# Last mask ahead of the w_down issues, a transposing DMA at positions 6 to 14

## What is computed

```python
def rmsnorm(x, g):
    y = x32 * lax.rsqrt(jnp.mean(x32 * x32, axis=-1, keepdims=True) + EPS) * g
...
def block(x, ...):
    u, q, k, v, o, ig, lf = mixer_inputs(x, norm1, w_in, b_gate)   # rmsnorm(x, norm1) @ w_in
    pool_out = pool_mix(u_ext, pos, w_pool, pool_scale)            # windows 2, 4, 8, 16
    h, mstate = run_mlstm(q, k, v, ig, lf)                         # chunked matrix memory, 4 heads of 128
    x = x + mixer_output(pool_out, h, o, head_gain, w_out, x.dtype)
    x = x + channel_mixer(x, norm2, w_up, w_down)                  # relu(rmsnorm(x, norm2) @ w_up)**2 @ w_down
```

## Time and profile before

| what | value |
|---|---|
| runs, us | 801.2 median of 3 (799.27 to 801.76) |
| profiled execution | 800.4 us, of which the span of the slowest core (core 2) is 799.3 us |
| spans of the 8 cores | 793.3 to 799.3 us |
| PE busy | 763.3 us, 95% of the span |
| DVE, ACT, POOL busy | 433.6, 365.8, 158.1 us |
| chain that ended last | PE 76%, DMA 10%, DVE 7%, POOL 3% |

### The profile page before, as it was taken

How to read it: one execution, slowest core, us unless ns; L and a number is a source line. 1 busy time by engine, 2 the same in 40 slices (tenths; PEclk the granted TensorE clock), 3 DMA queues, 4 the chain that set the end, 5 groups by cost and what they waited for, 6 DMA issues and landing times.

```text
span 799.3 us, 17270 instructions; the slowest of 8 cores (793.3 to 799.3 us)
## 1 busy us (share of the span) xinstructions
PE 763.3 (95%) x7001; PEld 540.4 (68%) x7001; DVE 433.6 (54%) x955; ACT 365.8 (46%) x872; POOL 158.1 (20%) x243
## 2 busy tenths in 40 slices
PE   6799999999999999999999859999999999999996
PEld 5587777877787787878788747778744446444443
DVE  3466886788876856877875446324324243421212
ACT  4455786777795745787684424313211010101102
POOL 7533321443332020320233010100001121100000
PEclk8978999999999999999999979999999999999999
DMA  9999995427241212132128966961377647553411
GB/s 146 179 198 172 189 207 123 88 48 183 66 118 64 94 69 88 44 120 85 64 82 138 177 133 214 164 167 69 116 243 278 219 148 257 188 187 121 182 52 53
DMA packets 35862, 110.47 MB, mean 138 GB/s; under 512 B 3431, under 2 KB 6871, under 8 KB 31798
## 3 DMA queue, kind: packets, MB, share of 16 engines
q1 hardware_dynamic: 21150, 63.31, 23.9%
q0 software_dynamic: 9648, 29.20, 22.7%
q10 hardware_dynamic: 4984, 16.86, 5.6%
HBM read 96.41 MB, written 39.64 MB: 170 GB/s over the span
## 4 chain that ended last, share of the span: by engine, by line
PE 76%; DMA 10%; DVE 7%; POOL 3%; issue 2%; ACT 2%; POOLq 0%; DVEq 0%; ACTq 0%
PE B L428 73%; DMA wdn<-w_down 5%; DMA hgB<-head_gain 4%; PE B L431 2%; DVE zt L437 1%; DVE ast L434 1%; POOL Wa L448 1%; DVE mixh L437 1%; POOL Wb L448 1%; DVE xt L434 1%; DVE qs L434 1%; DVE xn2T L434 0%; DVE xnT L434 0%; POOL og L448 0%; DVE Pt L434 0%
## 5 line engine op out<-in xcount | busy, mean ns | idle before, releaser
L428 PE MATMUL B<-xn2T,wup 128*128 128x256 bf16 (+1 forms) x2304 | 246.4, 264 | 0.7 <-ACT numS L425 0.3
L428 PEld LDWEIGHTS B<-xn2T,wup 128*128 128x128 bf16 x2304 | 204.5, 98 | 25.9 <-issue 0.7
L428 PE MATMUL B<-wdn,aTl 128*128 128x512 bf16 x896 | 199.2, 379 | 0.0
L428 PEld LDWEIGHTS B<-wdn,aTl 128*128 128x128 bf16 x896 | 87.0, 98 | 103.9
L434 DVE TENSOR_TENSOR ast<-rr 128x512 bf16<-128x512 f32 x132 | 97.2, 736 | 69.5 <-ACT rr L425 58.8
L425 ACT ACTIVATE rr<-B 128x512 f32<-128x512 f32 x132 | 78.3, 594 | 110.5 <-PE B L428 95.0
L434 DVE TENSOR_TENSOR xt<-xt,B 128x512 f32<-128x512 f32 (+1 forms) x68 | 46.5, 683 | 146.8 <-PE B L428 145.5
L425 ACT ACTIVATE junk<-xt 128x1024 bf16<-128x1024 f32 (+2 forms) x18 | 18.2, 1009 | 187.6 <-DVE xt L434 187.6
L428 PE MATMUL B<-w_out_sb,mixT 128*128 128x512 bf16 (+1 forms) x272 | 62.8, 379 | 0.0
L425 ACT ACTIVATE xn<-xt 128x1024 bf16<-128x1024 f32 (+2 forms) x34 | 35.8, 1054 | 36.5 <-DVE xt L434 27.5
L448 POOL TENSOR_TENSOR kz<-ktm,wsm 64x512 bf16<-64x512 bf16 x16 | 16.4, 1038 | 179.7 <-PE B L428 158.3
(11 more groups left out here) (211 smaller groups left out, 984.4 us busy)
## 6 DMA issues: line engine op xcount, KB each, us to landing
aTd<-ast SPq DMA_DIRECT2D x32, 512.0 KB, 3.7
aTl<-aTd SPq DMA_DIRECT2D x16, 1024.0 KB, 6.8
wup<-w_up POOLq DMA_DIRECT2D x8, 1024.0 KB, 36.1
x2d<-xt SPq DMA_DIRECT2D x16, 512.0 KB, 3.5
xt<-x2d SPq DMA_DIRECT2D x16, 512.0 KB, 3.4
yp<-xt ACTq DMA_DIRECT2D x15, 512.0 KB, 3.8
wdn<-w_down POOLq DMA_DIRECT2D x7, 1024.0 KB, 13.0
xt<-xp SPq DMA_DIRECT2D x12, 512.0 KB, 4.9
```

What stands on the lines that cost most here:

```text
L428: return lambda: nc.tensor.matmul(out, lhsT=lhsT, rhs=rhs, start=start, stop=stop)
```

## The change

Four edits. (1) The affine select of position 16 (i = 15) also writes a key `dtlast`, and the issues of `wdn3` and later have to wait for it, so that in POOL's order it stands ahead of them. (2) In `pre` at positions 6 to 14, and in `tail` at positions 6 to 13 (tiles 5 to 12), `trT` is left out: a DMA from ACT's queue transposes `xn` straight into `xnT` or `xn2T`, and DVE multiplies that tile by the gain in place. These are 9 and 8, together 17 of the 34 transposes of a tile. (3) The planner books 1.2 us of ACT for such an issue and 400e3 bytes for its 256 KB. (4) PRE, FRONT and POOLP, the due times of `pre`, `front` and the windowed sums, are moved from -100, 0 and 10 to -50, 20 and 0, which shifts the planned order on all engines.

```diff
-PRE, FRONT, MID, TAIL, POOLP, OGP = -100, 0, 30, -80, 10, 60
+PRE, FRONT, MID, TAIL, POOLP, OGP = -50, 20, 30, -80, 0, 60
+TX0, TX1, TX2 = 6, 13, 14
...
-                free[o.eng] = o.start + (1.0 if q == 'sw' else 0.3 if o.eng == 'act' else 0.4)
+                free[o.eng] = o.start + (1.0 if q == 'sw' else o.cost if o.cost > 1.0 else 0.3 if o.eng == 'act' else 0.4)
...
+        def XPOSE(prio, out, in_, R, W, chan):
+            pl.add('act', [lambda: nc.scalar.dma_start_transpose(out=out, in_=in_)], R, W, 1.2, prio, chan, 400e3, 512)
...
-            T = trT(pr, 128)
-            V(pr, vtt(X[:], Bb[T]..., gcol1..., ALU.mult), [bk(T), 'gvec'], [xk], 1.2)
+            if not TX0 <= pos <= TX2:
+                T = trT(pr, 128)
+                V(pr, vtt(X[:], Bb[T]..., gcol1..., ALU.mult), [bk(T), 'gvec'], [xk], 1.2)
+            else:
+                XPOSE(pr, X[:], xn[:], ['xn'], [xk], 'tx%d' % ix(pos))
+                V(pr, vtt(X[:], X[:], gcol1..., ALU.mult), [xk, 'gvec'], [xk], 1.2)
...
-            asel(pr, Dt[:], [[0, 4], [1, 128]], ALU.is_ge, 0, -1, 'Dt', cG(512))
+            G(pr, lambda: nc.gpsimd.affine_select(out=Dt[:], ...), ['Dt'], ['Dt'] + (['dtlast'] if i == 15 else []), cG(512))
...
-            T = trT(pr, n)
+            X2 = xn2T[gs][:, :, half * 128:half * 128 + n]
+            if sp_ or not TX0 <= pos <= TX1:
+                T = trT(pr, n)
+                V(pr, vtt(X2, Bb[T]..., gB, ALU.mult), [bk(T), 'gvec'], [xnk], 1.2)
+            else:
+                XPOSE(pr, X2, xn[:], ['xn'], [xnk], 'ty%d%d' % (gs, half))
+                V(pr, vtt(X2, X2, gB, ALU.mult), [xnk, 'gvec'], [xnk], 1.2)
...
-            DMA(1650 + u, 'pool', t[:], ..., ['wdn%d' % (u - 2)] if u > 1 else [], ['wdn%d' % u], ...)
+            DMA(1650 + u, 'pool', t[:], ..., (['wdn%d' % (u - 2)] if u > 1 else []) + (['dtlast'] if u > 2 else []), ['wdn%d' % u], ...)
```

More of the change, by code:

```diff
@@ L856, in pre @@
             norm(pr, xt[xs_][:], 'xt%d' % xs_, st[s2], 'st%d' % s2, 128)
-            T = trT(pr, 128)
-            V(pr, vtt(X[:], Bb[T].rearrange("p (k t) -> p k t", k=8), gcol1.unsqueeze(2).to_broadcast([128, 8, 128]), ALU.mult),
-              [bk(T), 'gvec'], [xk], 1.2)
+            if not TX0 <= pos <= TX2:
+                T = trT(pr, 128)
+                V(pr, vtt(X[:], Bb[T].rearrange("p (k t) -> p k t", k=8), gcol1.unsqueeze(2).to_broadcast([128, 8, 128]), ALU.mult),
+                  [bk(T), 'gvec'], [xk], 1.2)
+            else:
+                XPOSE(pr, X[:], xn[:], ['xn'], [xk], 'tx%d' % ix(pos))
+                V(pr, vtt(X[:], X[:], gcol1.unsqueeze(2).to_broadcast([128, 8, 128]), ALU.mult), [xk, 'gvec'], [xk], 1.2)
         def front(pos):
@@ L942, in mid @@
             A(pr, act(interB[:], src[:, :, :], AF.Exp, scale=-1.0), [sk, 'Dt'], [ibk], cA(512))
-            asel(pr, Dt[:], [[0, 4], [1, 128]], ALU.is_ge, 0, -1, 'Dt', cG(512))
+            G(pr, lambda: nc.gpsimd.affine_select(out=Dt[:], in_=Dt[:], pattern=[[0, 4], [1, 128]], compare_op=ALU.is_ge, fill=0.0,
+                                                  base=0, channel_multiplier=-1), ['Dt'], ['Dt'] + (['dtlast'] if i == 15 else []), cG(512))
             V(pr, vtt(qs[:], qT[s2][:], interB[:], ALU.mult), [qk_, ibk], ['qs'], cV(512))
@@ L1023, in tail @@
             norm(pr, x_[r_, :], xk, st[2 + pos % 2], sk, n)
-            T = trT(pr, n)
             gs, half = (0, 0) if sp_ else ((i // 2) % 2, i % 2)
             xnk = 'xn2T%d%d' % (gs, half)
-            V(pr, vtt(xn2T[gs][:, :, half * 128:half * 128 + n], Bb[T].rearrange("p (k t) -> p k t", k=8)[:, :, r_],
-                      gcol2.unsqueeze(2).to_broadcast([128, 8, n]), ALU.mult), [bk(T), 'gvec'], [xnk], 1.2)
+            X2 = xn2T[gs][:, :, half * 128:half * 128 + n]
+            gB = gcol2.unsqueeze(2).to_broadcast([128, 8, n])
+            if sp_ or not TX0 <= pos <= TX1:
+                T = trT(pr, n)
+                V(pr, vtt(X2, Bb[T].rearrange("p (k t) -> p k t", k=8)[:, :, r_], gB, ALU.mult), [bk(T), 'gvec'], [xnk], 1.2)
+            else:
+                XPOSE(pr, X2, xn[:], ['xn'], [xnk], 'ty%d%d' % (gs, half))
+                V(pr, vtt(X2, X2, gB, ALU.mult), [xnk, 'gvec'], [xnk], 1.2)
         for gs in range(2):
@@ L1130, in build @@
             wdn.append(t)
-            DMA(1650 + u, 'pool', t[:], w_dn_v[:, 4 * u:4 * u + 4, :], ['wdn%d' % (u - 2)] if u > 1 else [], ['wdn%d' % u], 'Lwdn%d' % u, 2048e3)
+            DMA(1650 + u, 'pool', t[:], w_dn_v[:, 4 * u:4 * u + 4, :], (['wdn%d' % (u - 2)] if u > 1 else []) + (['dtlast'] if u > 2 else []), ['wdn%d' % u], 'Lwdn%d' % u, 2048e3)
         NA = 3
```

## The result

The changed kernel takes **789.7 us** (median; 789.18 to 790.87), the one before 801.2 in the same rounds: ratio 0.9876, 95% interval 0.985 to 0.9901, so 1.0 to 1.5% faster. Medians here leave out the executions in which the cores of one die ran at a visibly lower clock, as one of the kernel before did in these rounds, at 879.57 us. The time lies in the range, 5 us above the forecast of 784.7: the gain is 11.5 us where 16.5 were expected. The profiled execution took 790.9 us, its slowest core (core 0) 789.8; over the 8 cores the mean span went from 796.1 to 784.5.

What follows compares the result with a forecast made beforehand. PE was taken as the bound, busy 763.3 of 799.3 us. 799.3 - 11.9 - 7.6 + 3.0 = 782.8 us of span, 784.7 us as the median of runs; range 778 to 797.

Steps and rivals of the forecast that it cites:

- part 1: Last mask on POOL, freed from the wait of wdn4: PE's wait for Pt and the cold restart go, 11.9 us.
- part 3: Shifted due times on all engines: no work added or removed, 0 with 2 us either way.
- part 2: 17 tile transposes leave PE at 0.45 us each: 7.6 us won, 3 us set against it.
- I cost this at nothing: wdn3 and wdn4 issued behind the mask: their first reader, down, comes late enough, so 0 us.
- The 10.0 us: PE's single wait for DVE's Pt ahead of the last chunk: goes whole or nearly so.
- the clock's 1.9: Matmuls after PE's restart at 467.33 us, partly at the lower clock: 1.9 us won at full clock.
- the 3 us set aside: Waits for transposing DMAs at the 17 places, landings of 4 to 6 us: 0.2 us for each.
- They move rows and add or remove no work: Due times, rows of all engines: PE's order the same up to the first w_q matmuls, so 0 us.
- The wait that stays ahead of the mask: Rival: wdn2, waiting for wdn0, still delays the mask; stall of 5 us, 787 to 790 us; chance 0.10.
- The DMA that is late: Rival: DVE waits at 17 multiplications and PE stops; decides from landings of about 6.8 us, comes out slower; chance 0.10.
- More is won: Rival: the order also closes some of PE's other 26 us of idle, 777 to 781 us; chance 0.06.
- under 1 us of idle per 50 us: Sign on PE: idle below this in each stretch from 150 to 400 us.

Runs made afterwards that it cites:

- e4: Kernel before with only the hold (key dtlast) added: 792.44 us, ratio 0.9915.
- e3: The change with the old due times, so hold and transposes only: 785.15 us, ratio 0.9815.
- e6: Kernel before with only the transposing DMAs added: 791.16 us, ratio 0.9896.
- e8: Kernel before with only the new due times: 800.27 us, ratio 1.0001.
- e2: The change without the transposing DMAs, so hold and new due times only: 808.31 us, ratio 1.0103.
- e1: The change without the hold (key dtlast), so transposes and new due times only: 796.72 us, ratio 0.9961.
- e7: e3 with every transposing DMA issued twice, the second behind the landing of the first: 842.28 us, ratio 1.0526.
- e11: e3 with transposing DMAs at positions 4 to 15, 23 tiles in place of 17: 819.40 us, ratio 1.0236.
- e5: e3 with PRE alone at its new value, -50: 790.29 us, ratio 0.9887.
- e9: e3 with the hold only from wdn4 on, wdn3 free again: 791.11 us, ratio 0.9889.

## Why the prediction was right, and where not

**Right in its verdict and in the mechanism of both parts.** The wait ahead of the last chunk is gone for the reason given, the transposes left PE at the price given, and 789.7 lies between 778 and 797. That the time came within 5 us of the forecast owes something to luck: part 1 fell 4 us short and part 3 cost 4.6 that nobody had set down, while part 2 brought 2.7 more than forecast. Measured by parts, with the forecast beside:

| term | forecast | measured |
|---|---|---|
| part 1, the mask | -11.9 | -7.7 (kernel before to e4) |
| part 2, the transposes, with what they give back | -7.6 + 3.0 = -4.6 | -7.3 (e4 to e3) |
| part 3, the due times | 0 ± 2 | +4.6 (e3 to the change) |
| sum | -16.5 | -10.4 |

The kernel before was at 800.1 in the rounds of e4 and at 801.2 in those of the change, which is the rest to the 11.5 above. Each difference carries some 2 to 3 us of noise, so 7.3 against the forecast 4.6 of part 2 is hardly a difference, while the shortfall of part 1 and the cost of part 3 are. The three add up on this path only, as the full set shows (us):

| | no hold | hold |
|---|---|---|
| kernel before | 800.1 | 792.4 (e4) |
| transposes | 791.2 (e6) | 785.2 (e3) |
| due times | 800.3 (e8) | 808.3 (e2) |
| transposes and due times | 796.7 (e1) | 789.7 (the change) |

The hold brings 6 to 8 us in three of the rows and costs 8 in one. The transposes bring 9 on the kernel before and 19 on the one with mask and due times. Where a part moves the planner's order, its price is that of the new order and not of the work it takes away.

**Part 1.** The step that failed is "I cost this at nothing", said of `wdn3` and `wdn4` behind the mask; the term of 11.9 us came out as 7.7. I looked for their reader, `down`, and it wasn't held up, as forecast. I did not ask what else is on the DMA engines when they load. `wdn4` now runs together with a store of `ast` that had no such load beside it; `ast` has a writer that waits, and so about 3 us of idle plus matmuls at the lower clock came back at 480 to 510 us (e4: 3.4 us of idle; the change: 2.95). In e2 the same collision costs more than the hold wins. The 10.0 us and the clock's 1.9 were won in their own place: 460 to 480 us reads 19.95 at 1.00. With the transposes in, though, the wait to be won is no longer this one: e6 and e1 have 4.0 and 3.4 us of it left, most of that for the mask of position 15 behind `wdn3`, and by POOL's order the hold's 6 to 7 us there come from moving `wdn3`; no run has that move alone.

**Part 2.** The price of a tile on PE held: 7.6 us less of busy time were forecast. Core 0 shows 9.7, but its trace has 190 matmul records less where 17 x 8 = 136 left, so 54 of them are missing records; on the six cores with full records PE is busy 8.0 us less (762.0 to 754.0 by the mean), and 8.1 less from e4 to e3. The gain in place costs DVE nothing: 1217 ns against 1218. ACT spends 1.25 us on each issue, and no run prices that by itself; all of PE's waits for ACT's `xn` sum to 2.9 us in the change and 1.6 before. The landings were 2.9 and 4.7 us by their medians (2.7 to 4.7 and 2.7 to 6.6), where I had 4 to 6, so little of the 3 us set aside was needed: in the rows of the change DVE waited for a transposing DMA once, 1.2 us. e7 shows that at least some 1.3 us of lateness more would have been hidden. Two rules of the Trainium skill stood against each other here. Eight blocks one after the other at the figure of "VectorE: DVE Perf Modes", § The three transpose paths, would be an estimated 10.5 us; the trace does not agree, with 2.9. The Trainium skill's other page, "Advanced Engine Details and Errata", § X-Bar Transpose (TRN2), has such a DMA as fast as a regular one, and that fits the rows of the same size. The 31.93 us of e11 fit neither: plain transfers of twice the size beside it took 12.5 and 13.0.

**Part 3.** The step that failed is "They move rows and add or remove no work", and so 0. It was argued from the 6.8 us of idle in the first 20, where the order is the same; from 40 to 60 us, where it isn't, I had read no row. The filler moved away there is the 5 us, by e5 and by the first `up` matmul, which comes 4.6 us later than in e3. ± 2 was far too narrow as well: of four settings of these numbers on the same work, the times are 785, 790, 790 and 816.

**The rivals.** The wait that stays ahead of the mask did not come in the change (`wdn0` landed after 15.0 us where this rival needed 16.6, so by 1.6 us), but e9 shows it, at position 15 and with the mechanism named: a load that shares the engines with another and lands late. The DMA that is late is real too, outside the range of positions chosen. "More is won" did not come: even e3, the best version, stands at 785.

**What would show it.** Met: `Pt`, the mask behind `wdn2`'s issue, PE busy down by some 8 us. Not met: under 1 us of idle per 50 us from 200 to 250, which has 1.4.

## What to carry to other kernels

When an issue or a load is moved out of the way, ask for more than its reader: list what else uses the DMA engines at its new time, and whose buffer waits for that. Look at all cores: the collision of this change shows on two of eight, and those two set the time. A DMA in place of engine work is worth its place only where the DMA engines have room; the same 256 KB landed in 2.9 us in one stretch and in 31.9 in another, so choose the range of tiles by the DMA share of each stretch. And time each part of a change apart: due times that looked like a harmless shift cost 5 us of the 15 that the other two parts had won.

## What the runs showed of the hardware

- A transposing DMA of 128x1024 in bf16 from SBUF to SBUF: 1.25 us of issue on ACT, 2.7 us to landing at the least. It adds some 1056 packets (53813 - 35862 over 17), all under 512 bytes.
- With w_up loads at a DMA share of 1.01, one of them took 31.93 us to land (31.9 to 36.0 over the 8 cores of e11), and plain transfers of 512 KB 12.5 and 13.0 us.
- Stores of 512 KB with a median of 4.1 us took 12.61 and 14.78 us beside loads of w_down; the first took 3.6 us in the kernel before, which has no such load there.
- Four gaps of 0.5 to 1.9 us within 8 us at the start went with a granted clock of 0.74 from 40 to 60 us (0.71 to 0.83 over the cores; 0.91 to 1.00 in e3, whose gaps sum to 1.2 us), and 8 matmuls took 3.62 us in place of 1.91, the lower of the two levels.
- A multiplication by DVE of 128x1024 in bf16 takes the same out of PSUM as out of SBUF in place, 1218 and 1217 ns.
